# First shift and scale of an adaptive-norm block, moved from VectorE's multiply-adds to one-column products on TensorE

## The chip, the cores and the metric

The kernel runs on one core of a Trainium2 chip. The metric is the device time of one launch in microseconds (us). The core has five engines that work side by side and meet at semaphores: TensorE (PE, with its weight loads shown as PEld), VectorE (DVE), ScalarE (ACT), GpSimd (POOL) and SyncE (SP), which here issues the weight transfers.

## The reference

Two transformer blocks on 256 tokens of width 2048, in f32. The first is conditioned by a vector `c`; the second has none. What matters here is the first lines of the first block:

```
cond = jax.nn.silu(c)                                   # (1, 2048)
mod = cond @ w_ada[i] + b_ada[i]                        # (1, 2048) @ (2048, 12288)
shift1, scale1, gate1, shift2, scale2, gate2 = jnp.split(mod, N_MOD, axis=-1)
h = _modulate(_rms(x, norm1_w[i]), shift1, scale1)      # y * (1 + scale) + shift
proj = h @ w_in[i]                                      # (256, 2048) @ (2048, 4096)
```

Then come a state-space mixer, a dilated attention, the output projection with `gate1`, a gated feed-forward with `shift2`, `scale2`, `gate2`, and the second block (feed-forward, input projection, pooling and attention, output projection, feed-forward). `shift1` and `scale1` are the first 4096 columns of `w_ada`. `proj` needs both, so nothing of the large products can start before them.

## The kernel before

All weights are read once, in tiles of 1 MB: 4 k-tiles of 128 rows by 512 columns, `raw[0..3]`, a ring of four buffers. SyncE issues their transfers in the order of the phases (`stream`, L349 to L385); before each it waits until the tile that was in the buffer four tiles earlier has been used (`used`, L350). A tile of kind "S" is split for a product of f32 in parts: ACT writes the rounded `w_hi` (L396), VectorE `w_lo = raw - w_hi` (L401), and TensorE multiplies three times, `w_hi` with the high and low part of the activations and `w_lo` with the high part (L494 to L496). A tile of kind "V" belongs to `w_ada` and is not split: VectorE multiplies it by `cond` and adds it up (`condition`, L404 to L415). There `cond` is stored as 128 partitions by 16 columns, so that one k-tile has one factor in each partition. After 16 k-tiles of a column group of 512, the accumulator holds 128 partial sums per column, and `gather` (L417 to L421) sums them over the partitions: four products on TensorE with 128 columns of the accumulator as the stationary operand and one column of ones as the moving one, each written to one column of the accumulation memory. The result stands with the model dimension over the partitions, as the norm needs it.

Phases (L255 to L272): `ada1` first, 8 column groups of 4 "V" tiles each, which are `shift1` and `scale1`. Then `w_in`, whose order mixes two "S" tiles with one "V" tile (`gate1`), `attn` with 16 "V" tiles (`scale2`), and so on; `shift2` and `gate2` are mixed into `w_out` and the first feed-forward. Only `ada1` stands alone: nothing of `w_in` can run on TensorE until it is through.

The opening block (L729 to L834) has one program for each engine:

- ACT loads `x`, makes `cond` with a Silu (L756), copies the transposed `x` into `res` (L760), and squares it in four quarters (L587), waiting after each for VectorE's reduction.
- VectorE runs groups 0 and 1 of `ada1`, then the four reductions of the squares (L593), groups 2 to 4 in a loop, the root of the norm (L543, L545), groups 5 to 7 in a loop. Then it waits for the last gather (L795), adds the bias to give `mod` (L797), makes the norm's gain (L799, L801) and goes into `w_in` with the norm's scaling (L560, L573, L574).
- TensorE transposes vectors and `x` (L808 to L820). Then it does the eight gathers, each when VectorE's group is complete, with the norm's sum over partitions (L518) behind the fourth, and goes into the products of `w_in`.

The order on each engine is that of its program; there is no planner. In each loop the group index is a register.

Of the kernel before, what the change touches and what calls it, by code (L numbers as in the profile page):

```python
# [24 lines left out]
P = 128  # L25
D = 2048
KT = D // P
# [116 lines left out]
def build(nc, a, out):  # L144
# [4 lines left out]
    with stack:  # L149
# [51 lines left out]
        badain = at("badain", [96, P], offset=hid_at + 24576 + 512)  # L201
        outb = at("outb", [P, 2, D], offset=hid_at)

        acc1 = at("acc1", [P, 8, GROUP], offset=proj_at)
        accg1 = at("accg1", [P, 4, GROUP], offset=hid_at)
        accs2 = at("accs2", [P, 4, GROUP], offset=act_at + 17408)
        accg2 = at("accg2", [P, 4, GROUP], offset=proj_at)
# [78 lines left out]
        const_in, vec_in, x_in, mix_in = sem("const_in"), sem("vec_in"), sem("x_in"), sem("mix_in")  # L286
        x_t, vec_t, vec_copied, cond_ready, mod_ready = sem("x_t"), sem("vec_t"), sem("vec_copied"), sem("cond_ready"), sem("mod_ready")
        res_in, acc_step, mod_sum, mod_read = (sem(n) for n in ("res_in", "acc_step", "mod_sum", "mod_read"))
        ssm_pre, par_t = sem("ssm_pre"), sem("par_t")
        ssm_tables, e_ready, bt_ps, bt_ready, ct_ps, ct_ready = (sem(n) for n in (  # L290
            "ssm_tables", "e_ready", "bt_ps", "bt_ready", "ct_ps", "ct_ready"))
# [50 lines left out]
        def loop(eng, start, end, body):  # L342
# [3 lines left out]
            elif end > start:  # L346
                with eng.Fori(start, end) as i:
                    body(i)

        def used(p, it, j):  # L350
            n = p.nth(it, j) + 1
            return {"S": (lo_ready, n), "V": (acc_step, CK * n)}[p.order[j]]

        def stream(sp, name, head=True, rest=True):

# [48 lines left out]
        def condition(dve, p, it, j, acc, c):  # L404

            landed(dve, p, it, j)
            v = p.nth(it, j)
            for t in range(CK):
                w, x = raw[j % RING][:, t, :], cond[:, CK * c + t:CK * c + t + 1]
                if not (isinstance(v, int) and v == 0 and t == 0):  # L410
                    dve.wait_ge(acc_step, CK * v + t)
                if c == 0 and t == 0:
                    dve.tensor_scalar(acc, w, x, None, ALU.mult).then_inc(acc_step, 1)
                else:
                    dve.scalar_tensor_tensor(out=acc, in0=w, scalar=x, in1=acc, op0=ALU.mult, op1=ALU.add).then_inc(acc_step, 1)  # L415

        def gather(pe, acc, bank_, col):  # L417

# [261 lines left out]
        def gate2_pe(pe):  # L680
            p = byname["ffn1.up0"]
            pe.wait_ge(bank_free[0], group_index(byname["ffn1.down0"], 0, 0))
            for g in range(4):
                pe.wait_ge(acc_step, CK * (p.before["V"] + 4 * g + 4))
                gather(pe, accg2[:, g, :], 0, 4 * g)
            pe.wait_ge(mod_read, 1)

        def gate2_dve(dve):
            dve.wait_ge(mod_sum, 24)
            dve.tensor_tensor(mod[:, GATE2:GATE2 + 16], ps[:, 0, 0:16], bada[:, GATE2:GATE2 + 16], ALU.add).then_inc(mod_read, 1)  # L690
            dve.wait_ge(mod_read, 1)

# [37 lines left out]
        with block:  # L730
# [43 lines left out]
            @block.vector  # L774
            def _(dve):
                dve.memset(half_pi[:, :], HALF_PI)
                dve.wait_ge(cond_ready, 1)

                def ada_body(it):
                    for j in range(4):  # L780
                        condition(dve, byname["ada1"], it, j, acc_of(acc1, it), j)
                ada_body(0)
                ada_body(1)
                for q in range(QUADS):
                    squares_dve(dve, q, q)
                loop(dve, 2, 5, ada_body)
                root_dve(dve, "norm1")
                loop(dve, 5, 8, ada_body)
                dve.wait_ge(vec_copied, 2)
                scale = float(P) ** -0.5  # L790
                dve.tensor_scalar(qk_gain[:, 0:1], vecs[:, V_QK:V_QK + 1], scale, None, ALU.mult)
                dve.tensor_copy(qk_gain[:, 1:2], vecs[:, V_QK + 1:V_QK + 2])
                dve.tensor_scalar(qk_gain[:, 2:3], vecs[:, V_QK + 2:V_QK + 3], scale, None, ALU.mult)
                dve.tensor_copy(qk_gain[:, 3:4], vecs[:, V_QK + 3:V_QK + 4])
                dve.wait_ge(mod_sum, 8)  # L795

                dve.tensor_tensor(mod[:, 0:32], ps[:, 5, 0:32], bada[:, 0:32], ALU.add).then_inc(bank_free[1], 1)  # L797
                dve.wait_ge(bank_free[1], 1)
                dve.tensor_scalar(gain[:, :], mod[:, 16:32], 1.0, None, ALU.add).then_inc(bank_free[0], 1)  # L799
                dve.wait_ge(bank_free[0], 1)  # L800
                link(dve, "dve", dve.tensor_tensor(gain[:, :], gain[:, :], vecs[:, V_N1:V_N1 + 16], ALU.mult))  # L801
                run_phase(dve, "w_in", split_lo, nothing, lambda second: norm_dve(dve, "norm1", gain, 0, 0, second), accg1, norm=True)

            @block.tensor
            def _(pe):
                pe.wait_ge(const_in, 16)
                pe.wait_ge(vec_in, 16 * 13)
                pe.transpose(ps[:, 7, 0:V_ROWS], vin[:, :], ident[0:V_ROWS, 0:V_ROWS]).then_inc(vec_t, 1)  # L808
                pe.transpose(ps[:, 7, P:P + 96], badain[:, :], ident[0:96, 0:96]).then_inc(vec_t, 1)
                pe.wait_ge(x_in, 32)  # L810
                for q in range(QUADS):
                    if q >= 2:
                        pe.wait_ge(res_in, q - 1)
                    for t in range(4):
                        for h in range(2):
                            mm = pe.transpose(ps[:, 2 * (q % 2) + t // 2, (t % 2) * SEQ + P * h:(t % 2) * SEQ + P * h + P],
                                              xin[:, h, P * (4 * q + t):P * (4 * q + t) + P], ident)
                    mm.then_inc(x_t, 1)
                for t in range(KT):
                    mm = pe.transpose(ps[:, 6, META * t:META * t + META], metain[:, P * t:P * t + P], ident[0:META, 0:META])  # L820
                mm.then_inc(x_t, 1)
                for g in range(8):
                    pe.wait_ge(acc_step, 4 * CK * (g + 1))
                    gather(pe, acc1[:, g, :], 5, 4 * g)
                    if g == 3:
                        norm_pe(pe, "norm1")
                products(pe, "w_in", act_hi, act_lo, SEQ_COLS, counted(act_ready, ACT0["norm1"]))


# [76 lines left out]
        with block:  # L906
# [129 lines left out]
            def _(dve):  # L1036
# [44 lines left out]

                dve.wait_ge(mix_in, SSM_IN)
                dve.wait_ge(pre_act, 8)
                dve.wait_ge(mod_sum, 12)
                dve.tensor_tensor(mod[:, GATE1:GATE1 + 16], ps[:, 5, P:P + 16], bada[:, GATE1:GATE1 + 16], ALU.add)

                def z(i):
# [312 lines left out]
        with block:  # L1400
            @block.sync
            def _(sp):
                sp.dma_start(sel[:, :, :], a["sel"].rearrange("a (h p) -> a h p", h=HEADS)).then_inc(mix_in, 16)
                sp.dma_start(dil[:, :], a["dilated"]).then_inc(mix_in, 16)
                stream(sp, "attn", head=False)
                stream(sp, "glu")

            @block.scalar
            def _(act):
                v_act(act, 0)  # L1410
                units_act(act, 0)

            @block.vector
            def _(dve):
                dve.wait_ge(mix_in, SSM_IN + 32)
                p = byname["attn"]
                units_dve(dve, 0, lambda s_: condition(dve, p, 0, s_, accs2[:, s_ // 4, :], s_ % 4) if s_ < p.body else None)
                dve.wait_ge(mod_sum, 16)
                link(dve, "dve", dve.tensor_tensor(mod[:, SCALE2:SCALE2 + 16], ps[:, 5, 0:16], bada[:, SCALE2:SCALE2 + 16], ALU.add))
                link(dve, "dve", dve.tensor_scalar(gain[:, :], mod[:, SCALE2:SCALE2 + 16], 1.0, None, ALU.add))  # L1420
                link(dve, "dve", dve.tensor_tensor(gain[:, :], gain[:, :], vecs[:, V_N2:V_N2 + 16], ALU.mult))

            @block.tensor
            def _(pe):
                pe.wait_ge(mix_in, SSM_IN + 32)
                v_pe(pe, 0)

                def conditioning(s_):

                    if s_ in (4, 8, 12, 16):  # L1430
                        g = s_ // 4 - 1
                        pe.wait_ge(acc_step, CK * (byname["attn"].before["V"] + 4 * g + 4))
                        gather(pe, accs2[:, g, :], 5, 4 * g)

                units_pe(pe, 0, conditioning)
# [32 lines left out]
        with block:  # L1468
# [27 lines left out]
            def _(dve):  # L1496
# [8 lines left out]
                pend = run_phase(dve, "w_out", split_lo, bind(dve, gate1), pend, accb2)  # L1505

                def shift2():
                    dve.wait_ge(mod_sum, 20)
                    dve.tensor_tensor(mod[:, SHIFT2:SHIFT2 + 16], ps[:, 1, 0:16], bada[:, SHIFT2:SHIFT2 + 16], ALU.add)

                pend = ffn_dve(dve, "ffn1", then(pend, shift2, lambda second: norm_dve(dve, "norm2", gain, 0, 48, second)), add_dve(("mod", 80)),
# [6 lines left out]
            def _(pe):  # L1518
# [2 lines left out]
                p = byname["w_out"]  # L1521
                pe.wait_ge(bank_free[0], group_index(p, 1, 0) + 1)
                for g in range(4):
                    pe.wait_ge(acc_step, CK * (p.before["V"] + 4 * g + 4))
                    gather(pe, accb2[:, g, :], 1, 4 * g)
                norm_pe(pe, "norm2")
                ffn_pe(pe, "ffn1", ACT0["norm2"])
# [178 lines left out]
```

## Time and profile before

| | us |
|---|---|
| median of 3 runs | 3633.84 (3631.2 to 3637.37) |
| profiled execution, span from first to last instruction | 3632.1 |
| TensorE busy | 3259.9 (90%) |
| VectorE busy | 2023.8 (56%) |
| ScalarE busy | 1203.8 (33%) |
| `cond` written | at 14.2 of the span |
| `mod` written for shift and scale | at 130.3 |
| first product of `w_in` starts | at 138.9 |

The profiled execution's own time is known by its span, 3632.1 us; the runs without a profile have a median 1.7 us above it. Times in the trace count from the first instruction. A row of a timeline gives start, length, engine, source line, operation, output and inputs, and the number of instructions; several of one kind in a row are one row. [...] An f32 product shows as two loads and two passes, so two records on each of PEld and PE.

### The profile page before, as it was taken

The numbers are of one execution on the slowest core, as the hardware profiler recorded it, in microseconds if no ns is written. First come the engines' busy times: TensorE is split into PE (matmuls) and PEld (weight loads), VectorE is DVE, ScalarE is ACT, GpSimd is POOL, SyncE is SP. The second block draws the span as 40 slices with busy tenths as digits, with TensorE's granted clock in tenths as the row PEclk, the third lists the DMA queues.
The fourth block names the chain that finished last, engine by engine and source line by source line (L and its number), as shares of the span: only waits on it lengthen the run. The fifth ranks groups of instructions, "written<-read, shape, count | busy, mean of one in ns | idle before, by whom it ended". The sixth has DMA issues, their size and how long they took to land. (4 is left out here: it accounts for less than half of the span.)

```text
span 3632.1 us, 57499 instructions
## 1 busy us (share of the span) xinstructions
PE 3259.9 (90%) x24952; PEld 3123.1 (86%) x24952; DVE 2023.8 (56%) x1942; ACT 1203.8 (33%) x1068; POOL 161.8 (4%) x120
## 2 busy tenths in 40 slices
PE   2597565788999999989999999989989899999999
PEld 2496333688999999989999999989947899999999
DVE  7865998887754444464444444463334644444444
ACT  1233332233333333333333333333333333333333
POOL 0000652000000000000000000003000000000000
PEclk6798555699999999999999999999967999999999
DMA  8785002585755555545555555557702455555554
GB/s 298 261 278 175 0 0 98 197 306 199 267 200 186 186 187 187 188 144 178 175 176 176 175 174 174 173 138 173 179 0 96 149 188 187 186 187 188 185 185 139
DMA packets 328668, 630.02 MB, mean 173 GB/s; under 512 B 22324, under 2 KB 24008, under 8 KB 328280
## 3 DMA queue, kind: packets, MB, share of 16 engines
q1 hardware_dynamic: 328104, 626.00, 53.8%
q10 hardware_dynamic: 448, 2.39, 0.2%
q8 instruction: 82, 1.34, 0.2%
q14 instruction: 34, 0.28, 0.0%
HBM read 626.26 MB, written 2.10 MB: 173 GB/s over the span
## 5 line engine op out<-in xcount | busy, mean ns | idle before, releaser
L401 DVE TENSOR_TENSOR w_lo<-raw,w_hi 128x2048 fp32r<-128x2048 f32 x496 | 1138.5, 2296 | 1375.2 <-ACT w_hi L396 1374.8
L494 PE MATMUL ps<-act_hi,w_hi 128*128 128x256 f32 (+1 forms) x5760 | 1640.1, 285 | 73.4 <-DVE act_lo L574 43.0
L495 PE MATMUL ps<-act_lo,w_hi 128*128 128x256 f32 (+1 forms) x5760 | 1638.6, 284 | 0.0
L496 PE MATMUL ps<-act_hi,w_lo 128*128 128x256 f32 (+1 forms) x5760 | 1636.7, 284 | 0.0
L396 ACT ACTIVATE w_hi<-raw 128x2048 fp32r<-128x2048 f32 x496 | 950.2, 1916 | 1903.5 <-PE ps L496 1853.5
L494 PEld LDWEIGHTS ps<-act_hi,w_hi 128*128 128x128 f32 x5760 | 1094.7, 190 | 79.2 <-issue 48.5
L495 PEld LDWEIGHTS ps<-act_lo,w_hi 128*128 128x128 f32 x5760 | 1094.3, 190 | 0.0
L496 PEld LDWEIGHTS ps<-act_hi,w_lo 128*128 128x128 f32 x5760 | 1093.4, 190 | 0.0
L494 PE MATMUL ps<-hid_hi,w_hi 128*128 128x256 f32 (+1 forms) x2176 | 617.2, 284 | 11.9 <-DVE w_lo L401 8.6
L496 PE MATMUL ps<-hid_hi,w_lo 128*128 128x256 f32 (+1 forms) x2176 | 616.6, 283 | 0.0
L495 PE MATMUL ps<-hid_lo,w_hi 128*128 128x256 f32 (+1 forms) x2112 | 598.5, 283 | 0.0
L494 PEld LDWEIGHTS ps<-hid_hi,w_hi 128*128 128x128 f32 x2176 | 412.1, 189 | 12.7 <-issue 12.7
L496 PEld LDWEIGHTS ps<-hid_hi,w_lo 128*128 128x128 f32 x2176 | 411.5, 189 | 0.0
L495 PEld LDWEIGHTS ps<-hid_lo,w_hi 128*128 128x128 f32 x2112 | 398.4, 189 | 0.0
L1187 PE MATMUL ps<-hh,ct 128*128 128x256 f32 x128 | 62.6, 641 | 53.8 <-POOL hh L952 53.8
L1187 PEld LDWEIGHTS ps<-hh,ct 128*128 128x128 f32 x128 | 36.4, 314 | 76.2 <-POOL hh L952 70.8
L420 PE MATMUL ps<-const,acc 128*128 128x1 f32 x64 | 14.9, 355 | 92.2 <-DVE acc L415 92.2
L420 PEld LDWEIGHTS ps<-const,acc 128*128 128x128 f32 x64 | 14.3, 328 | 93.6 <-DVE acc L415 93.6
L415 DVE SCALAR_TENSOR_TENSOR acc<-raw,cond,acc 128x512 f32 (+1 forms) x120 | 90.2, 752 | 4.7
L1546 POOL TENSOR_TENSOR win<-proj 128x542 f32<-128x542 f32 x4 | 7.3, 1833 | 1914.6 <-ACT proj L602 1914.3
L415 DVE SCALAR_TENSOR_TENSOR accg<-raw,cond,accg 128x512 f32 (+1 forms) x120 | 90.1, 751 | 3.4
L1179 PE MATMUL ps<-ui,bt 32*128 32x256 f32 x128 | 61.3, 643 | 2.0 <-DVE t L1114 1.9
(230 smaller groups left out, 1645.1 us busy)
## 6 DMA issues: line engine op xcount, KB each, us to landing
raw<-in_w_ada SPq DMA_DIRECT2D x96, 1024.0 KB, 5.1
raw<-in_ffn_w_gate SPq DMA_DIRECT2D x88, 1024.0 KB, 5.2
raw<-in_ffn_w_up SPq DMA_DIRECT2D x88, 1024.0 KB, 5.2
raw<-in_ffn_w_down SPq DMA_DIRECT2D x88, 1024.0 KB, 5.1
raw<-in_w_in SPq DMA_DIRECT2D x64, 1024.0 KB, 5.9
raw<-in_w_ffn_gate SPq DMA_DIRECT2D x44, 1024.0 KB, 5.2
raw<-in_w_ffn_up SPq DMA_DIRECT2D x44, 1024.0 KB, 5.2
raw<-in_w_ffn_down SPq DMA_DIRECT2D x44, 1024.0 KB, 5.1
```

Of the source, the lines that this page charges most:

```text
L396: act.activation(w_hi[b][:, :, :], raw[j % RING][:, :, :], ACT.Copy).then_inc(hi_ready, 1)
L401: dve.tensor_tensor(w_lo[b][:, :, :], raw[j % RING][:, :, :], w_hi[b][:, :, :].bitcast(F32), ALU.subtract).then_inc(lo_ready, 1)
L415: dve.scalar_tensor_tensor(out=acc, in0=w, scalar=x, in1=acc, op0=ALU.mult, op1=ALU.add).then_inc(acc_step, 1)
L420: mm = pe.matmul(ps[:, bank_, col + m:col + m + 1], acc[:, P * m:P * m + P], ones[:, 0:1], start=True, stop=True, skip_group_check=True)
L494: pe.matmul(o, whi, hi[:, k, cols], start=(k == 0), stop=False)
L495: pe.matmul(o, whi, lo[:, k, cols], start=False, stop=False)
L496: mm = pe.matmul(o, wlo, hi[:, k, cols], start=False, stop=(k == CK * p.cpg - 1))
L1179: mm = pe.matmul(ps[:, b, SEQ * r:SEQ * r + SEQ], bt[rows_, parity, r, :], ui[rows_, parity, :], start=True, stop=True)
L1187: mm = pe.matmul(ps[:, 4 + 2 * parity, 0:SEQ], ct[:, parity, r, P * jj:P * jj + P], hh[:, b, r, :], start=(jj == 0 and r == 0), stop=(jj = ...
L1546: link(pool, "pool", pool.tensor_tensor(dst[:, :, w - 1:T], src[:, :, w - 1:T], src[:, :, w // 2 - 1:T - w // 2], ALU.add))
```

## The change

For `ada1` alone, the raw weight tile itself becomes the stationary operand, 128 by 128 at a time, and a column of `cond` the moving one. The 16 k-tiles are added up in the accumulation memory, in bank 5, where the gathers used to write. So a tile of 4 k-tiles by 512 columns is 16 products, and nothing is left for VectorE to multiply or for TensorE to gather in this phase. The new semaphore `mod_step` is raised once for each tile; SyncE waits on it before it refills a buffer, and VectorE waits for all 32 before it writes `mod`. The norm's sum over partitions now stands behind the first column group. Groups 1 to 7 are a loop on TensorE, in which the output column is addressed through a register. VectorE runs the four reductions and the root with no `ada1` between them. The counts of `acc_step` and `mod_sum` in the later phases are lowered by what `ada1` no longer adds. The later "V" tiles stay as they are.

```diff
--- before.py
+++ after.py
@@ -201,7 +201,6 @@
         badain = at("badain", [96, P], offset=hid_at + 24576 + 512)
         outb = at("outb", [P, 2, D], offset=hid_at)
 
-        acc1 = at("acc1", [P, 8, GROUP], offset=proj_at)
         accg1 = at("accg1", [P, 4, GROUP], offset=hid_at)
         accs2 = at("accs2", [P, 4, GROUP], offset=act_at + 17408)
         accg2 = at("accg2", [P, 4, GROUP], offset=proj_at)
@@ -286,6 +285,7 @@
         const_in, vec_in, x_in, mix_in = sem("const_in"), sem("vec_in"), sem("x_in"), sem("mix_in")
         x_t, vec_t, vec_copied, cond_ready, mod_ready = sem("x_t"), sem("vec_t"), sem("vec_copied"), sem("cond_ready"), sem("mod_ready")
         res_in, acc_step, mod_sum, mod_read = (sem(n) for n in ("res_in", "acc_step", "mod_sum", "mod_read"))
+        mod_step = sem("mod_step")
         ssm_pre, par_t = sem("ssm_pre"), sem("par_t")
         ssm_tables, e_ready, bt_ps, bt_ready, ct_ps, ct_ready = (sem(n) for n in (
             "ssm_tables", "e_ready", "bt_ps", "bt_ready", "ct_ps", "ct_ready"))
@@ -347,9 +347,13 @@
                 with eng.Fori(start, end) as i:
                     body(i)
 
+        ADA1 = byname["ada1"].iters * byname["ada1"].body
+
         def used(p, it, j):
             n = p.nth(it, j) + 1
-            return {"S": (lo_ready, n), "V": (acc_step, CK * n)}[p.order[j]]
+            if p.name == "ada1":
+                return mod_step, n
+            return {"S": (lo_ready, n), "V": (acc_step, CK * (n - ADA1))}[p.order[j]]
 
         def stream(sp, name, head=True, rest=True):
 
@@ -404,7 +408,7 @@
         def condition(dve, p, it, j, acc, c):
 
             landed(dve, p, it, j)
-            v = p.nth(it, j)
+            v = p.nth(it, j) - ADA1
             for t in range(CK):
                 w, x = raw[j % RING][:, t, :], cond[:, CK * c + t:CK * c + t + 1]
                 if not (isinstance(v, int) and v == 0 and t == 0):
@@ -413,6 +417,19 @@
                     dve.tensor_scalar(acc, w, x, None, ALU.mult).then_inc(acc_step, 1)
                 else:
                     dve.scalar_tensor_tensor(out=acc, in0=w, scalar=x, in1=acc, op0=ALU.mult, op1=ALU.add).then_inc(acc_step, 1)
+
+        def project(pe, it, bank_):
+
+            p = byname["ada1"]
+            for j in range(p.body):
+                landed(pe, p, it, j)
+                for t in range(CK):
+                    k = CK * j + t
+                    for m in range(4):
+                        o = ps[:, bank_, 4 * it + m:4 * it + m + 1] if isinstance(it, int) else ps[:, bank_, bass.ds(4 * it + m, 1)]
+                        mm = pe.matmul(o, raw[j][:, t, P * m:P * m + P], cond[:, k:k + 1], start=(k == 0 and m == 0),
+                                       stop=(k == KT - 1), skip_group_check=True)
+                mm.then_inc(mod_step, 1)
 
         def gather(pe, acc, bank_, col):
 
@@ -681,12 +698,12 @@
             p = byname["ffn1.up0"]
             pe.wait_ge(bank_free[0], group_index(byname["ffn1.down0"], 0, 0))
             for g in range(4):
-                pe.wait_ge(acc_step, CK * (p.before["V"] + 4 * g + 4))
+                pe.wait_ge(acc_step, CK * (p.before["V"] - ADA1 + 4 * g + 4))
                 gather(pe, accg2[:, g, :], 0, 4 * g)
             pe.wait_ge(mod_read, 1)
 
         def gate2_dve(dve):
-            dve.wait_ge(mod_sum, 24)
+            dve.wait_ge(mod_sum, 16)
             dve.tensor_tensor(mod[:, GATE2:GATE2 + 16], ps[:, 0, 0:16], bada[:, GATE2:GATE2 + 16], ALU.add).then_inc(mod_read, 1)
             dve.wait_ge(mod_read, 1)
 
@@ -776,23 +793,16 @@
                 dve.memset(half_pi[:, :], HALF_PI)
                 dve.wait_ge(cond_ready, 1)
 
-                def ada_body(it):
-                    for j in range(4):
-                        condition(dve, byname["ada1"], it, j, acc_of(acc1, it), j)
-                ada_body(0)
-                ada_body(1)
                 for q in range(QUADS):
                     squares_dve(dve, q, q)
-                loop(dve, 2, 5, ada_body)
                 root_dve(dve, "norm1")
-                loop(dve, 5, 8, ada_body)
                 dve.wait_ge(vec_copied, 2)
                 scale = float(P) ** -0.5
                 dve.tensor_scalar(qk_gain[:, 0:1], vecs[:, V_QK:V_QK + 1], scale, None, ALU.mult)
                 dve.tensor_copy(qk_gain[:, 1:2], vecs[:, V_QK + 1:V_QK + 2])
                 dve.tensor_scalar(qk_gain[:, 2:3], vecs[:, V_QK + 2:V_QK + 3], scale, None, ALU.mult)
                 dve.tensor_copy(qk_gain[:, 3:4], vecs[:, V_QK + 3:V_QK + 4])
-                dve.wait_ge(mod_sum, 8)
+                dve.wait_ge(mod_step, ADA1)
 
                 dve.tensor_tensor(mod[:, 0:32], ps[:, 5, 0:32], bada[:, 0:32], ALU.add).then_inc(bank_free[1], 1)
                 dve.wait_ge(bank_free[1], 1)
@@ -819,11 +829,10 @@
                 for t in range(KT):
                     mm = pe.transpose(ps[:, 6, META * t:META * t + META], metain[:, P * t:P * t + P], ident[0:META, 0:META])
                 mm.then_inc(x_t, 1)
-                for g in range(8):
-                    pe.wait_ge(acc_step, 4 * CK * (g + 1))
-                    gather(pe, acc1[:, g, :], 5, 4 * g)
-                    if g == 3:
-                        norm_pe(pe, "norm1")
+                pe.wait_ge(cond_ready, 1)
+                project(pe, 0, 5)
+                norm_pe(pe, "norm1")
+                loop(pe, 1, 8, lambda it: project(pe, it, 5))
                 products(pe, "w_in", act_hi, act_lo, SEQ_COLS, counted(act_ready, ACT0["norm1"]))
 
 
...
```

What is left out is the same shift of counts in the later phases (`mod_sum` by 8, `acc_step` by `CK * ADA1`).

## Rows read from the trace of the kernel before

**Rows 1.** The page: busy time of two engines, then their digits in 40 slices.

```profile
PE 3259.9 (90%) x24952; PEld 3123.1 (86%) x24952; DVE 2023.8 (56%) x1942; ACT 1203.8 (33%) x1068; POOL 161.8 (4%) x120
...
PE   2597565788999999989999999989989899999999
...
DVE  7865998887754444464444444463334644444444
```

**Rows 2.** Timeline of the opening stage, 0 to 160 us (start, length, instruction, count).

```profile
12.02 6.05 PE L816 MATMUL ps<-const,xin 128*128 128x128 f32 x32
...
13.98 0.22 ACT L756 ACTIVATE cond<-vecs 128x16 f32<-128x16 f32 x1
...
14.75 11.98 DVE L415 SCALAR_TENSOR_TENSOR acc<-raw,cond,acc 128x512 f32<-128x512 f32 x15
...
18.00 1.16 PE L820 MATMUL ps<-const,metain 16*128 16x16 f32 x16
...
39.25 1.99 DVE L593 TENSOR_REDUCE ssq<-sig 128x272 f32<-128x1088 f32 x1
...
50.66 0.48 DVE L413 TENSOR_SCALAR acc<-raw,cond 128x512 f32 x1
51.17 11.78 DVE L415 SCALAR_TENSOR_TENSOR acc<-raw,cond,acc 128x512 f32 x15
...
77.18 3.97 PE L518 MATMUL ps<-ssq,const 128*128 128x272 f32 x8
87.76 0.43 DVE L543 TENSOR_SCALAR rtmp<-ps 128x272 f32<-128x272 f32 x1
...
128.21 5.26 SPq L380 DMA_DIRECT2D raw<-in_w_in  x2
...
128.23 1.87 PE L420 MATMUL ps<-const,acc 128*128 128x1 f32 x8 [10.58 <-DVE acc L415]
...
130.14 0.19 DVE L797 TENSOR_TENSOR mod<-ps,bada 128x32 f32<-128x32 f32 x1 [1.72 <-PE ps L420]
...
138.92 0.57 PE L494 MATMUL ps<-act_hi,w_hi 128*128 128x256 f32 x1 [8.81 <-DVE act_lo L574]
```

**Rows 3.** Waits of SyncE's queue, 0 to 400 us (total us, times, longest).

```profile
SPq L380 <- DVE acc L415: 99.0, 32, 13.3
```

**Rows 4.** Windows of 1 us (length; PE, PEld, DVE, ACT, POOL busy; PEclk; DMA; GB/s).

```profile
18.00:19.00 1.00, 1.00 (x17) 1.00 (x16) 0.96 (x2) 1.00 (x2) 0.00 (x0) 1.00 1.05 387
...
20.00:21.00 1.00, 0.00 (x0) 0.00 (x0) 0.90 (x2) 0.72 (x1) 0.00 (x0) 0.66 1.05 383
```

**Rows 5.** Timeline of TensorE around the three later bursts of gathers.

```profile
335.40 4.86 PE L420 MATMUL ps<-const,accg 128*128 128x1 f32 x32
...
821.09 3.63 PE L420 MATMUL ps<-const,accb 128*128 128x1 f32 x32
824.58 3.03 PE L518 MATMUL ps<-ssq,const 128*128 128x272 f32 x8
...
1028.55 2.18 PE L420 MATMUL ps<-const,accg 128*128 128x1 f32 x19
...
1030.73 2.70 PE L420 MATMUL ps<-const,accg 128*128 128x1 f32 x12
```

**Rows 6.** Windows at those bursts and behind the norm's sum at 77 us.

```profile
337.00:338.00 1.00, 1.00 (x11) 1.00 (x10) 0.53 (x2) 0.45 (x3) 0.00 (x0) 0.88 0.00 0
...
825.00:826.00 1.00, 1.00 (x6) 0.66 (x4) 1.00 (x1) 0.56 (x1) 0.00 (x0) 0.93 0.00 0
...
1031.00:1032.00 1.00, 1.00 (x6) 1.00 (x7) 1.00 (x1) 0.00 (x0) 0.00 (x0) 0.50 0.93 354
...
80.00:100.00 20.00, 3.02 (x11) 2.12 (x9) 18.35 (x24) 0.43 (x1) 0.00 (x0) 0.59 0.85 284
```

**Rows 7.** Timeline of ScalarE, 120 to 165 us: the split of the fourth transferred tile.

```profile
147.97 1.90 ACT L396 ACTIVATE w_hi<-raw 128x2048 fp32r<-128x2048 f32 x1
```

**Rows 8.** Instructions of SyncE's line L380, 0 to 135 us (ns min/median/max).

```profile
L380 SPq FUSED_REGOPS  x28: 37/37/48, 17.1 to 115.8; - x28
```

More of the change, by code:

```diff
@@ L1083, in _ @@
                 dve.wait_ge(pre_act, 8)
-                dve.wait_ge(mod_sum, 12)
+                dve.wait_ge(mod_sum, 4)
                 dve.tensor_tensor(mod[:, GATE1:GATE1 + 16], ps[:, 5, P:P + 16], bada[:, GATE1:GATE1 + 16], ALU.add)
@@ L1417, in _ @@
                 units_dve(dve, 0, lambda s_: condition(dve, p, 0, s_, accs2[:, s_ // 4, :], s_ % 4) if s_ < p.body else None)
-                dve.wait_ge(mod_sum, 16)
+                dve.wait_ge(mod_sum, 8)
                 link(dve, "dve", dve.tensor_tensor(mod[:, SCALE2:SCALE2 + 16], ps[:, 5, 0:16], bada[:, SCALE2:SCALE2 + 16], ALU.add))
@@ L1431, in conditioning @@
                         g = s_ // 4 - 1
-                        pe.wait_ge(acc_step, CK * (byname["attn"].before["V"] + 4 * g + 4))
+                        pe.wait_ge(acc_step, CK * (byname["attn"].before["V"] - ADA1 + 4 * g + 4))
                         gather(pe, accs2[:, g, :], 5, 4 * g)
@@ L1507, in shift2 @@
                 def shift2():
-                    dve.wait_ge(mod_sum, 20)
+                    dve.wait_ge(mod_sum, 12)
                     dve.tensor_tensor(mod[:, SHIFT2:SHIFT2 + 16], ps[:, 1, 0:16], bada[:, SHIFT2:SHIFT2 + 16], ALU.add)
@@ L1523, in _ @@
                 for g in range(4):
-                    pe.wait_ge(acc_step, CK * (p.before["V"] + 4 * g + 4))
+                    pe.wait_ge(acc_step, CK * (p.before["V"] - ADA1 + 4 * g + 4))
                     gather(pe, accb2[:, g, :], 1, 4 * g)
```

## The prediction, as put on record before the kernel ran

> **What bounds the kernel now.** I read four views in this order. First the page's totals [rows 1]: TensorE is busy 90% of the 3632.1 us, so over the whole kernel it is the bound; but in the digits of its second part the first three or four slices are thin on PE and thick on DVE. So the stage that the change touches has another limit than the average. Second the timeline of that stage [rows 2]. VectorE's chain runs from `cond` (ready 14.2 us) through eight column groups of `ada1`, each one scale and 15 multiply-adds; one group is 0.48 + 11.78 us and the steps between, 12.4. Between the groups stand two interludes: four reductions of the squares (39.25 to 50.66, 11.4 us) and the root (from 87.76, about 3 us). 14.2 + 8 x 12.4 + 11.4 + 3 = 127.8, the trace has 128.1 as the end of VectorE's part; the last gather on TensorE ends at 130.1, and `mod` is added at 130.14. Everything after (gain, norm, first product at 138.92) hangs on that. TensorE has almost nothing to do before: eight bursts of gathers. Third SyncE's waits [rows 3] and the windows [rows 4]: the 32 weight tiles of 1 MB are issued when VectorE lets a buffer go (32 waits, 99.0 us), and where nothing holds them back the transfers move about 387 GB/s, which is 2.7 us a tile, against VectorE's 3.1. Transfers are near, but not the limit. Fourth the gathers themselves at both clocks [rows 5, 6], since the new work has their form.
>
> So the stage is a serial chain ending in `mod`, and a microsecond more or less before `mod` is a microsecond of the span, as long as what follows keeps its distance.
>
> **What the change removes.** Eight times 16 operations on VectorE (0.48 + 11.78 us a time, 98 us [rows 2]) and the gathers: the whole stretch from 14.2 to 130.1 is replaced. The interludes leave the path too: VectorE is idle, so the squares (ACT is ready for them at 19.6; one square of 1.1 us and the 11.4 of now) are through at about 32, and the root waits for its sum on TensorE only. The eight gathers of `ada1`, 64 records, go.
>
> **What it adds.** Per tile 16 products: stationary 128x128 of the raw weight, one moving column. 32 tiles give 512 products. A gather is exactly this form (128x128 f32 stationary, 128x1 out), and four gather products make 8 records: two weight loads and two passes each. So 1024 records. Their pace is read start to start, since loads and passes overlap. At full clock 32 records take 821.09 to 824.58, 3.49 us, 0.109 us each. At half clock 12 records span 2.70 us, of which the last lasts 0.35 like any of them: 2.35 / 11 = 0.2136; the burst of eight at 128.23, 1.87 us, gives 1.52 / 7 = 0.217 [rows 5, 2]. So 0.427 us a product and 6.8 us a tile at half clock, 0.218 and 3.5 at full clock. VectorE took 3.1 us a tile. Everything turns on which clock is granted.
>
> **The clock.** The trace answers with three later bursts of 32 records in which TensorE never idled [rows 5, 6]. Products or sums of squares ran at full clock right before. [...] At 1028.55 they began, and it was at 0.50 in the slice from 1031 on; the rest ran at half clock and half pace. At 821.09 they began; here the burst was over at 824.6, the norm's sum followed at once, and the clock still fell at 825.9. The eight bursts in the stage itself are all at 0.50, and in none did it rise. I therefore take half clock for the new stream, with two exceptions. The clock shown at the start is 1.00 until 20.3 us (0.66 in the slice 20 to 21 [rows 4]), so 1.1 us of the stream runs at full. And the norm's sum of squares, 4.0 us of 272-column products at 77.18, was followed by a spell of full clock: 0.59 over the 20 us from 80 on, so 0.09 x 20 / 0.50 = 3.6 us [rows 2, 6]. In the new kernel it stands behind the first column group, so I grant 3.6 us there as well.
>
> [...]
>
> **The sum.** The stream starts behind the transposes, which end at 19.16 [rows 2]: 19.2. 1024 x 0.2136 = 218.7. The norm's eight records stand in the same queue: 4.0. Less 1.1 us of full clock at the start (ten records for five, 1.1 us saved), less the 3.6 us after the norm (33 records for 17, 3.4 us saved). 19.2 + 218.7 + 4.0 - 1.1 - 3.4 = 237.4, so `mod` comes at 237.5 where it came at 130.14: +107.4 us. Costed at nothing:
> - The transfers: 2.7 us a tile under 6.8. If the stream were at full clock they would still hide under 3.5.
> - The first tiles: VectorE ran through its first group from 14.2 us on without a pause for data (15 operations in 11.98 us), TensorE starts 5 us later and is slower.
> - Squares and root: done by 32 and about 53, under the stream.
> - The `w_in` tiles: buffers come free 6.8 us apart, so the first three are there early. The fourth is issued 1.9 us ahead of `mod` today (128.21 against 130.14), then just at `mod`. It lands within 6 us, and ACT splits it 17.8 us after `mod` (147.97 [rows 7]), so 10 us of slack remain.
> - The start of the `w_in` products: 8.8 us behind `mod` as now, at half clock for the first four microseconds as now.
> - Register work: in the loop the output column is an address from a register. The trace has no such product on TensorE. From below it is nothing, hidden in 0.427 us a product: VectorE's 15 multiply-adds take 11.98 us with fixed and 11.78 with register addresses [rows 2], and SyncE's register operations last 37 ns, at most 48 [rows 8]. From above, if a whole step of VectorE's, 0.785 us, were the sequencer's time, 448 products would cost (0.785 - 0.427) x 448 = 160 us; one exposed operation of 37 ns a product would cost 17. I take nothing, nearest to the two loops that agree.
>
> The profiled execution would go from 3632.1 to 3739.5 of span. The median of the runs shown, 3633.84, stands 1.7 us above that span, so I predict 3741.
>
> **The rivals.**
> - *Full clock throughout.* Speaks for it: TensorE has never had such a stream for over 5 us in this trace, so a longer one is not shown. Against: the falls out of full clock at 337.8 and before 1031 within a burst that never paused, and none of the bursts raised it. 19.2 + 1024 x 0.109 + 2.3 for the norm = 133.1, +3 us: 3637, which is no difference.
> - *Faster: the stream outruns the transfers.* It needs less than (130.1 - 19.2 - 4.0) / 512 = 0.209 us a product, below even the full-clock 0.218; that could be if a load and pass were paid once a product, as in the transposes (32 records for 32 at 12.02 [rows 2]), and at full clock. Then transfers decide: 36 MB (32 tiles of 1.05, 2.4 of the rest) at 387 GB/s from 5.8 us on are done at 99, last products at 101, 29 us saved: 3605. Against it: every gather shows two records.
> - *Slower still: something exposed in each product or loop turn*, the register work above: +17 us at one operation a product, 3758, up to 3900 at the far bound.
> - *The change doesn't take VectorE off the path*: not possible in the numbers, since no instruction of the old chain is left; only the wait for the last tile remains.
>
> **How the numbers follow.** Half clock as summed 0.86, full clock 0.06, outrunning the transfers 0.02, exposed overhead 0.06. In the likeliest case the pace (0.2136 or up to 0.217, 3.5 us), the two stretches of full clock (none, or one more: 3.4 us each) and the runs' own spread (3631.2 to 3637.4) give 3733 to 3749. For 8 in 10 I widen it to 3727 (three or four more such stretches) and 3758 (one exposed operation). A measurement of this kernel tells about 0.2%, 7 us, from no change. Slower takes the first and last cases: 0.93. Full clock is mostly within 0.2%: 0.05. Faster is the rest, 0.02.
>
> **What would show it.** Right: in the changed kernel's windows PE and PEld busy all through 20 to 237 us with granted clock 0.50, but for one stretch after the norm; the new line's records 512 x 2 at 0.21 us start to start; SyncE waiting on TensorE instead of VectorE, 6.8 us a tile; `mod` near 238; first product 8.8 us later; later stages shifted by 107 us and otherwise alike. Wrong: granted clock 1.00 in that stretch; PE idle between records of one tile, or at the turn of a loop; TensorE waiting for transfers; a fourth `w_in` tile that comes late.

## The result and the profile after

The changed kernel takes 3746.5 us, the median of 4 runs (3744.8 to 3748.2), against 3633.6 for the kernel before (3631.2 to 3637.4): a ratio of 1.031 (95% interval 1.0295 to 1.0325), 112.9 us slower. The forecast was 3741, within 3727 to 3758. The span of the profiled execution went from 3632.1 to 3746.4, 114.3 us more.

The page of the changed kernel, totals and digits, to be read against [rows 1]:

```profile
PE 3466.1 (93%) x25912; PEld 3330.5 (89%) x25912; DVE 1930.4 (52%) x1814; ACT 1204.0 (32%) x1068; POOL 161.8 (4%) x120
...
PE   8989856578899999998999999998989899999999
...
DVE  1036599878764444456444444455433644444444
```

VectorE lost 93 us of work and TensorE gained 206; in the first three slices the thin row is now VectorE's. The timeline of the opening stage, against [rows 2]:

```profile
14.59 0.21 ACT L773 ACTIVATE cond<-vecs 128x16 f32<-128x16 f32 x1
...
19.58 26.47 PE L430 MATMUL ps<-cond,raw 128*128 128x1 f32 x128
...
30.82 1.99 DVE L610 TENSOR_REDUCE ssq<-sig 128x272 f32<-128x1088 f32 x1 [1.18 <-ACT sig L604]
...
45.91 3.97 PE L535 MATMUL ps<-ssq,const 128*128 128x272 f32 x8
...
49.68 191.15 PE L430 MATMUL ps<-cond,raw 128*128 128x1 f32 x896
...
240.86 0.19 DVE L807 TENSOR_TENSOR mod<-ps,bada 128x32 f32<-128x32 f32 x1 [187.77 <-PE ps L430]
...
249.64 0.57 PE L511 MATMUL ps<-act_hi,w_hi 128*128 128x256 f32 x1 [8.81 <-DVE act_lo L591]
```

The two pieces of the stream hold 1024 records. The long one gives the pace: (191.15 - 0.35) / 895 = 0.2132 us a record, start to start. VectorE waits 187.8 us for it. `mod` comes 110.7 us later than before, and the first product of `w_in` stands 8.8 us behind `mod` in both kernels. The windows say what TensorE ran at, against [rows 4] and [rows 6]:

```profile
20.00:21.00 1.00, 1.00 (x10) 1.00 (x9) 0.00 (x0) 0.97 (x2) 0.00 (x0) 0.85 0.81 295
21.00:22.00 1.00, 1.00 (x6) 1.00 (x7) 0.68 (x1) 0.21 (x1) 0.00 (x0) 0.50 0.08 29
...
60.00:80.00 20.00, 20.00 (x95) 20.00 (x96) 0.00 (x0) 0.00 (x0) 0.00 (x0) 0.50 0.45 147
...
200.00:220.00 20.00, 20.00 (x96) 20.00 (x95) 0.00 (x0) 0.00 (x0) 0.00 (x0) 0.50 0.47 157
```

Both PE columns are full, 20.00 of 20, and the granted clock, PEclk in the windows, is 0.50 of the full one all the way; the clock fell 1.1 us after the stream had begun. A busy share of 100% in the two TensorE columns is here an engine at half speed. Transfers are at 0.45 to 0.47 of their time: they wait. SyncE's waits, against [rows 3], now name TensorE:

```profile
SPq L384 <- PE ps L430: 210.4, 32, 15.2
```

### The profile page after: what moved, and what is told of

It is laid out like the page before. It is cut to its first block and busy times, and to the rows that moved or that the text cites. A ratio compares the mean times of both kernels' runs of the same rounds, so it can differ in the third digit from the quotient of the medians.

```text
span 3746.4 us, 59213 instructions
## 1 busy us (share of the span) xinstructions
PE 3466.1 (93%) x25912; PEld 3330.5 (89%) x25912; DVE 1930.4 (52%) x1814; ACT 1204.0 (32%) x1068; POOL 161.8 (4%) x120
## 5 line engine op out<-in xcount | busy, mean ns | idle before, releaser
L430 PEld LDWEIGHTS ps<-cond,raw 128*128 128x128 f32 x1024 | 217.8, 332 | 0.3
L430 PE MATMUL ps<-cond,raw 128*128 128x1 f32 x1024 | 217.6, 351 | 0.0
L807 DVE TENSOR_TENSOR mod<-ps,bada 128x32 f32<-128x32 f32 x1 | 0.2, 192 | 187.8 <-PE ps L430 187.8
L610 DVE TENSOR_REDUCE ssq<-sig 128x272 f32<-128x1088 f32 x20 | 41.4, 2071 | 43.9 <-ACT sig L604 43.9
```

Source lines behind the costliest of these rows:

```text
L430: mm = pe.matmul(o, raw[j][:, t, P * m:P * m + P], cond[:, k:k + 1], start=(k == 0 and m == 0), stop=(k == KT - 1), skip_group_check=True)
L610: dve.tensor_reduce(o, sig[:, :, :].rearrange("p t n -> p n t"), AX_X, ALU.add).then_inc(ssq_ready, 1)
```

## The experiments

**The moving operand made 128 columns wide.** The loads stay, the clock may differ. What the width brings with it changes too: the groups alternate between two banks, VectorE picks its columns after each group, and the loop is unrolled.

```diff
- mm = pe.matmul(o, raw[j][:, t, P * m:P * m + P], cond[:, k:k + 1], ...
+ mm = pe.matmul(ps[:, 4 + g % 2, P * m:P * m + WIDE], raw[j][:, t, P * m:P * m + P],     # WIDE = 128
+                cond[:, k:k + 1].broadcast_to([P, WIDE]), ...
```

> The same 512 products, but each moves 128 copies of the column of cond instead of one, so that the passes carry work; the loads are the same. Groups alternate between two accumulation banks, VectorE picks one column of each 128 and adds the bias, the loop is unrolled. Theory A (the price is the clock): the granted clock stays at 1.00 through the stream, records stand 0.109 us apart, the stream ends at 19.6 + 111.6 + 2 to 4 for the norm = about 134, mod at 134 instead of 240.9, total 3637 to 3642. Rival B (the loads of a stream of this form have their pace whatever the clock): 0.21 us a record, mod near 241, total 3747. Rival C (wide passes become the limit): full clock, but a record dearer than 0.109; at 0.15 mod is at 176, total 3680.

Measured: 3640.3 us (10 runs), ratio 1.0021 (1.0012 to 1.0031). The timeline and the windows of this kernel:

```profile
34.56 100.21 PE L433 MATMUL ps<-cond,raw 128*128 128x128 f32 x896
...
134.81 0.16 DVE L442 TENSOR_TENSOR mod<-ps,bada 128x4 f32<-128x4 f32 x1 [14.13 <-PE ps L433]
```

```profile
60.00:80.00 20.00, 20.00 (x181) 20.00 (x180) 0.32 (x2) 0.00 (x0) 0.00 (x0) 1.00 0.87 287
80.00:100.00 20.00, 20.00 (x182) 20.00 (x180) 0.16 (x1) 0.00 (x0) 0.00 (x0) 1.00 0.92 303
```

TensorE is as full as before, but at granted clock 1.00, with nearly twice the records in a window. The pace is (100.21 - 0.27) / 895 = 0.1117 us a record. Multiplying 128 times as many columns made the stage 106 us shorter. The granted clock of this kernel is 1.00 in every window from the transposes to the stream's end at 134.8 us. That settles the cause of the price: the number of products and loads is the same, and the pace went with the clock that the chip granted to them. Of the other differences, the unrolled loop alone gave no such gain (next run), and the shared kernels further down alternate the same two banks with one-column products and run at 0.50 (the first of them from 25 to 114 us). Theory A held, and rival B fell. Of rival C a little is left: 0.1117 for 0.109 is 2.8 us over 1024 records. Of widths between 1 and 128 nothing was run.

At the same clock a record with 128 moving columns behind the same load took 2% longer than one with a single column: 0.1117 us against 0.109 [rows 5].

**The loop unrolled.**

```diff
- loop(pe, 1, 8, lambda it: project(pe, it, 5))
+ for it in range(1, 8):
+     project(pe, it, 5)
```

> The changed kernel with the loop over groups 1 to 7 unrolled on TensorE, so that no output address comes from a register. Theory A (register work is hidden): same to 1 us, 3746, mod at 241. Rival (part of the 0.2136 us a record is the sequencer's work on addresses): faster by 17 us or more, mod at 224 or earlier.

Measured: 3744.8 us (two runs, 3741.6 and 3748.0), ratio 1.031 (1.0289 to 1.033), which is the changed kernel's. No 17 us were gained, so register work is hidden to within the runs' spread. The changed kernel's own row for the line shows how little there is, four operations for each turn of the loop and none for each product:

```profile
L430 PEldq FUSED_REGOPS  x28: 46/46/60, 44.0 to 210.8; - x28
```

This run shows another thing. Its `mod` came at 237.05 instead of 240.86, and its windows behind the norm's sum tell why:

```profile
48.00:50.00 2.00, 2.00 (x17) 1.82 (x15) 0.69 (x2) 0.43 (x1) 0.00 (x0) 0.95 0.95 366
50.00:52.00 2.00, 2.00 (x19) 2.00 (x18) 1.95 (x5) 0.00 (x0) 0.00 (x0) 0.90 0.05 12
52.00:54.00 2.00, 2.00 (x11) 2.00 (x11) 0.00 (x0) 0.00 (x0) 0.00 (x0) 0.50 0.03 6
```

Here a spell of full clock began with the last records of the norm's sum; in the changed kernel's profiled execution there was none. The two kernels issue the same products there, and each was profiled once. So the 3.4 us that I had granted for it don't follow from the products alone; what decides on the spell is not shown.

**Most products left out**, to find the transfers' floor.

```diff
- for m in range(4):
+ for m in range(4 if k == 0 else 1):
```

> The changed kernel with most products left out: of the four column blocks of a tile only the first is multiplied, except in the first k-tile of a group (19 products a group instead of 64; the result lacks the rest). Theory A (the stream is records times pace, transfers are hidden until they decide): 8 x 19 x 2 = 304 records x 0.2136 = 65 us, less than the transfers need; the 36 MB decide, the last tile is done at about 100 to 103, total 3606 to 3610. Rival (a fixed price for each tile, by handing buffers back): total well above 3620, with TensorE idle between tiles while transfers are idle too.

Measured: 3611.2 us (3609.7 and 3612.8), ratio 0.9942 (0.9922 to 0.9962), just above what theory A gave. Three of four column blocks are left out, so this is not a version of the kernel, only a bound: `mod` at 106.72, TensorE idle 0.5 to 0.9 us before most tiles for a transfer, and from 60 us on the transfers at 387 GB/s without a gap:

```profile
60.00:80.00 20.00, 15.90 (x71) 15.39 (x71) 0.00 (x0) 0.00 (x0) 0.00 (x0) 0.50 1.05 387
```

A fixed price for each tile, with transfers idle, doesn't show. The last tile came at 104.8 instead of 100 to 103, because TensorE stood in the norm's sum until 32 us, waiting for VectorE's reductions, and held the ring meanwhile (266 GB/s from 20 to 40). So a stage that is fast enough may gain some 22 us over the kernel before, if it keeps the transfers going.

**Both engines share the tiles, whole tiles each.** Order in each group of four: VectorE, VectorE, TensorE, VectorE.

```diff
+ for g in range(8):                                # TensorE
+     for i in range(4 * g, 4 * g + 4):
+         if KINDS[i] == "P":
+             project(pe, i)                        # 16 products into bank 4 + g % 2
+         ...                                       # the norm's sum behind tile 10
+     if g:
+         gather1(pe, g - 1)                        # adds VectorE's sums, start=False
+ gather1(pe, 7)
```

> Both engines share the 32 tiles: in each group of four, TensorE multiplies the third as in the change, VectorE the other three as before; the gather adds VectorE's sums to TensorE's in the same accumulation columns. VectorE's reductions are spread between its tiles. Theory A (both stages are bound by one engine each, transfers have slack): VectorE has 24 x 3.11 + 8 + 3.2 = 86 us from 14.6 on, so to 101; TensorE 8 x 6.83 + 8 gathers of 1.75 + 4 = 73 us; transfers are done at 99.5. mod at 103 to 108, 22 to 27 us ahead of the kernel before, total 3607 to 3612. Rival (the ring of four couples the two: a slot held 6.8 us by TensorE starves VectorE): mod at 115 to 130, total 3620 to 3634.

Measured: 3617.6 us, ratio 0.9956 (0.9939 to 0.9972), faster than before but 6 us above the upper end of what theory A gave; `mod` at 114.1. The timeline of the period of four tiles:

```profile
79.41 6.99 PE L452 MATMUL ps<-cond,raw 128*128 128x1 f32 x32 [3.46 <-DMA raw<-in_w_ada]
82.10 3.11 DVE L442 SCALAR_TENSOR_TENSOR acc<-raw,cond,acc 128x512 f32<-128x512 f32 x4 [2.09 <-DMA raw<-in_w_ada]
...
91.50 6.99 PE L452 MATMUL ps<-cond,raw 128*128 128x1 f32 x32 [3.40 <-DMA raw<-in_w_ada]
```

Both engines wait for transfers, and the period is 91.50 - 79.41 = 12.1 us, where four transfers need 10.8. TensorE holds the third buffer for 6.99 us, and the next tile in that buffer stands ready 5.1 us after its issue at 86.42: 6.99 + 5.1 is the period. SyncE, which issues in the order of its program, can't refill the fourth before the third, though VectorE was done with it at 85.2; between 86 and 89 the transfers nearly stop (86 GB/s in the slice from 87 to 88). Part of the rival's coupling was real, at 1.3 us a group.

**Both engines share each tile**: three k-tiles for VectorE, one for TensorE.

```diff
- for t in range(CK):        # VectorE, in its tiles     (TensorE: all four t, in its tiles)
+ for t in range(KD):        # VectorE, KD = 3, in every tile
+ for t in range(KD, CK):    # TensorE, in every tile
```

> Each tile is shared instead of each group: of its four k-tiles VectorE takes three (2.35 us a tile), TensorE the fourth (4 products, 1.7 us at half clock), and the group's gather adds both in the same accumulation columns. A buffer is held by neither longer than a transfer takes. Theory A (the first shared kernel lost 7 us against the transfers because TensorE held every fourth buffer for 6.9 us and the transfers are issued in order): transfers decide now; mod at 105 to 108 instead of 114.1, total 3609 to 3613. Rival (the loss was contention, or VectorE's own load of 24 tiles): mod stays at 112 to 115, total 3616 to 3619.

Measured: 3614.1 us, ratio 0.9948 (0.9935 to 0.9962); `mod` at 109.88, between what theory A and the rival gave. The timeline shows a wait of VectorE for the norm's sum, which comes from where I had put the two, and the windows behind it show the transfers at 285 GB/s:

```profile
58.96 0.44 DVE L586 TENSOR_SCALAR rtmp<-ps 128x272 f32<-128x272 f32 x1 [3.84 <-PE ps L561]
```

```profile
60.00:80.00 20.00, 14.92 (x67) 14.49 (x68) 18.66 (x25) 0.00 (x0) 0.00 (x0) 0.50 0.80 285
80.00:100.00 20.00, 16.40 (x74) 15.89 (x74) 16.14 (x23) 0.00 (x0) 0.00 (x0) 0.50 1.05 389
```

**Order alone, nothing shared.** The kernel before, with the reductions spread between the tiles.

```diff
- ada_body(0); ada_body(1)
- for q in range(QUADS): squares_dve(dve, q, q)
- ...                                               # groups 2 to 4, root, groups 5 to 7
+ for i in range(32):
+     if i in [4, 6, 8, 10]: squares_dve(...)       # one reduction each
+     if i == 20: root_dve(dve, "norm1")
+     condition(dve, byname["ada1"], i // 4, i % 4, acc1[:, i // 4, :], i % 4)
```

> The kernel before, with nothing on TensorE but the gathers; only VectorE's four reductions are spread between its tiles (before the 5th, 7th, 9th and 11th), so that it doesn't wait for ScalarE's squares between them. It tells how much of the shared kernels' gain is order alone. If sharing is what gains: the interlude falls from 11.4 to 8 us, mod at 126 to 127, total 3629 to 3631. Rival (order was the loss): total below 3620.

Measured: 3630.2 us (11 runs), ratio 0.9993 (0.9984 to 1.0002), `mod` at 127.0, as expected. The total is not clear of noise; by the medians 2.4 us are order, by `mod` 3.1. The rest of the 18.5 us that the kernel before this one gained is sharing.

**The wait removed**: the norm's sum behind TensorE's 12th tile instead of the 14th, the root ahead of VectorE's 19th instead of its 15th.

```diff
- if i == 13: norm_pe(pe, "norm1")      # TensorE
+ if i == 11: norm_pe(pe, "norm1")
- if i == 14: root_dve(dve, "norm1")    # VectorE
+ if i == 18: root_dve(dve, "norm1")
```

> The tile-sharing kernel with the norm's sum two tiles earlier on TensorE and the root four tiles later on VectorE, so that VectorE doesn't wait for it (3.84 us at 58.96 before, after which the transfers ran at 285 instead of 387 GB/s for 20 us). Theory A (transfers decide, and that wait had stopped them): mod at 106 to 108 instead of 109.9, total 3609 to 3612. Rival (the transfers make up for a stop of that length by the ring): mod at 109 to 110, total unchanged at 3612 to 3615.

Measured: 3608.7 us (5 runs), ratio 0.9935 (0.9921 to 0.995), `mod` at 104.5, better than expected. Timeline and windows:

```profile
64.26 0.43 DVE L586 TENSOR_SCALAR rtmp<-ps 128x272 f32<-128x272 f32 x1
...
100.24 2.33 DVE L438 SCALAR_TENSOR_TENSOR acc<-raw,cond,acc 128x512 f32<-128x512 f32 x3 [0.32 <-DMA raw<-in_w_ada]
...
104.53 0.17 DVE L839 TENSOR_TENSOR mod<-ps,bada 128x16 f32<-128x16 f32 x1 [1.71 <-PE ps L456]
```

```profile
60.00:80.00 20.00, 16.80 (x77) 16.37 (x77) 18.27 (x25) 0.43 (x1) 0.00 (x0) 0.50 1.04 382
80.00:100.00 20.00, 16.52 (x75) 16.09 (x75) 16.50 (x23) 0.00 (x0) 0.00 (x0) 0.50 1.05 388
```

The transfers run at 1.04 from 40 us on, and from 82 us on VectorE waits 0.3 to 0.65 us for most tiles: the stage is bound by transfers. Against the previous sharing kernel the medians and `mod` both moved by 5.4 us, and 5.3 us is what 20 us at 285 instead of 387 GB/s lose; the intervals of the two ratios overlap, though, and each `mod` is of one execution. This kernel beats the one before by 0.65% and, by medians of runs that were not made side by side, the changed one by 3.7% (3608.7 / 3746.5 = 0.963). It runs the products of the change at granted clock 0.50 from 54 us to `mod`, 0.43 us each (four of them take 1.87 us), but so few of them that TensorE waits for transfers 11 times there, 8.4 us in all.

## Why the prediction was right

- *The bound.* Right: all before `mod` is a serial chain, and its delay of 110.7 us went through to the first product of `w_in`, 110.7 us later, with the same 8.8 us between.
- *The count.* Right: 1024 records on each of PE and PEld.
- *The pace at half clock.* Right: 0.2132 us measured against 0.2136 taken from 12 records of a gather [rows 5].
- *Which clock.* Right, and shown: the stream ran at 0.50, as the three falls from 1.00 at the gathers had told (at 337.8, at 825.9 and before 1031 [rows 6]), and the wide products show the same loads at 0.1117 us a record at granted clock 1.00. TensorE was busy for 221 us on end, all but the first 1.1 us at 0.50.
- *The two spells of full clock.* The first was right: 1.1 us of the stream by the window (19.58 to 20.7, from 0.85 in the slice at 20), as summed. The second, after the norm, was a term of 3.4 us that the profiled execution doesn't have; the range had allowed for none. 237.5 predicted, 240.9 measured: the spell gives +3.4, the later start (19.58 for 19.2) +0.4, the pace -0.4. The unrolled kernel had the spell and came in at 237.05.
- *Costed at nothing.* Squares done by 32.8 us and the root by 52.7, both hidden. Transfers hidden. The fourth `w_in` tile, now issued as `mod` is written, held nothing up: the first product and VectorE's first steps keep their distances.
- *Register work.* Right to take nothing: 28 operations of 46 ns, and no gain when unrolled.
- *The rest.* That later stages would shift alike was nearly right: of the 114.3 us of span, 3.6 arose behind the first product, for which the sum has no term. The first 1.5 us of them arose at one place, and the clock is what differs there. About the same stretch of `w_in` in the changed kernel and in the kernel before:

```profile
266.00:270.00 4.00, 4.00 (x21) 4.00 (x22) 3.93 (x4) 0.00 (x0) 0.00 (x0) 0.57 1.05 384
```

```profile
155.00:159.00 4.00, 3.76 (x32) 3.76 (x32) 3.93 (x5) 0.00 (x0) 0.00 (x0) 1.00 1.01 372
```

Granted clock 0.57 against 1.00, 21 records against 32, and VectorE's instructions stand 110.7 us apart before it and 112.25 behind it. Why the clock dipped in one and not in the other is not shown. Later the distance is 112.7 by the second feed-forward and between 113 and 115 behind that, in small steps; no experiment bears on these. The medians differ by 112.9 only. The missing spell (3.4) and this term (3.6) both made the change dearer: the span came out 6.9 us above the 3739.5 that were summed, the median 5.5 us above the forecast.

Of the rivals, full clock was priced at 3637 by the same sum. The wide products made it happen. Priced at 3 us slower than the kernel before, they measured 7.3 us slower beside it, 0.2%: at full clock the change would have been about level. The faster rival's floor, set by the transfers, was 29 us saved; the last kernel saved 24 by another way.

## What to carry to other kernels

A product with one moving column took nearly as long here as one with 128 behind the same load (0.109 against 0.1117 us a record at the same clock), and a stream of 1024 one-column records ran at granted clock 0.50 with TensorE busy for 221 us on end: read the granted clock beside the busy share, and find the smallest burst of the same form in the trace before trusting a count of instructions. Where moving work off an engine makes the other one the bound, share it so that both finish within a transfer, in slices small enough that neither holds a buffer longer than that (TensorE's 6.99 us on every fourth tile, against 2.7 for a transfer, cost 1.3 us a group here). And when order and size are tuned to the transfers, look for the first window in which their rate drops (here 285 instead of 387 GB/s from 60 us on); the wait that caused it stood just ahead (3.84 us, ended at 58.96).

## What the runs showed of the hardware

- Moving 128 columns instead of one behind each 128x128 f32 load nearly halved the time of the stream (0.1117 against 0.2132 us a record), with the granted clock at 1.00 instead of 0.50. I had expected full clock to be worth that much, but not that the wider passes would cost only 2% (0.1117 against 0.109).
- A spell of full clock (granted 1.00 after 0.50) behind four microseconds of 272-column products is not reproduced from one kernel to the next. It stands in the profiled executions of the kernel before (from 81.8 us), of the unrolled one (48.2), of the one with order alone (78.1) and of the last one (50.4), each time for three to four microseconds. It is missing in those of the changed kernel and of the first two sharing kernels, though the changed and the unrolled kernel issue the same products there.
